# Preparing the next weight chunk ahead of emptying the PSUM banks, in three small projections of a two-block transformer kernel

## The reference

```python
def mla_qkv(c_q, c_kv, k_r, g_q, w_uq, g_kv, w_ukv, angles):
    q = (rmsnorm_2(c_q, g_q) @ w_uq).reshape(B, L, MLA_HEADS, MLA_NOPE + MLA_ROPE)
    kv = (rmsnorm_2(c_kv, g_kv) @ w_ukv).reshape(B, L, MLA_HEADS, MLA_NOPE + MLA_V)
    q_nope, q_rope = q[..., :MLA_NOPE], q[..., MLA_NOPE:]
    k_nope, v = kv[..., :MLA_NOPE], kv[..., MLA_NOPE:]
    ...
    q_rope = axial_rope(q_rope, *angles)
    k_rope = axial_rope(k_rope, *angles)
```

## Time and profile before

| | |
|---|---|
| profiled execution, its own time | 2443.72 us |
| its span in the profile | 2442.1 us |
| median of 3 runs | 2444.67 us |
| busy: TensorE matmul / VectorE / ScalarE | 98% / 73% / 48% of the span |
| stretch of `uk`, `uv`, `uq` | about 1430 to 1529 us |

### The profile page before, as it was taken

The page is one execution under the profiler, slowest core; times in us unless marked ns, Lnnn a source line. Parts: engine busy times, 40 slices in busy tenths (PEclk is TensorE's granted clock), DMA queues, the critical chain, the costliest instruction groups (busy, mean ns, idle before and its releaser), DMA issues.

```text
span 2442.1 us, 42380 instructions
## 1 busy us (share of the span) xinstructions
PE 2401.3 (98%) x14850; PEld 2135.9 (87%) x14850; DVE 1774.2 (73%) x2868; ACT 1165.0 (48%) x1671; POOL 0.2 (0%) x4
## 2 busy tenths in 40 slices
PE   8999999999999999999999999899999999999998
PEld 8998899988888888889988978588888888888887
DVE  5676678798878888889776455457777567766775
ACT  5344445554545654445523333345565444444453
POOL 0000000000000000000000000000000000000000
PEclk9999999999999999999999999999999999999999
DMA  7775567588778876787468522044556555555553
GB/s 271 278 274 183 185 221 245 176 291 290 260 248 281 289 271 231 271 282 239 162 238 280 193 70 69 26 164 152 192 181 198 185 185 180 195 184 185 192 187 132
DMA packets 142644, 508.97 MB, mean 208 GB/s; under 512 B 15824, under 2 KB 19408, under 8 KB 142160
## 3 DMA queue, kind: packets, MB, share of 16 engines
q1 hardware_dynamic: 142544, 507.60, 60.7%
HBM read 505.44 MB, written 2.10 MB: 208 GB/s over the span
## 4 chain that ended last, share of the span: by engine, by line
PE 96%; DVE 2%; ACT 1%; issue 0%; DMA 0%; DVEq 0%; SPq 0%; ACTq 0%
PE ps L1034 42%; PE ps L1036 20%; PE ps L1059 8%; PE ps L1060 8%; PE ps L1061 8%; PE ps L1385 1%; PE ps L1033 1%; PE ps L1089 1%; PE ps L1091 1%; PE ps L1090 1%; PE ps L1203 0%; PE ps L1395 0%; PE ps L1404 0%; PE ps L1185 0%; PE ps L1184 0%
## 5 line engine op out<-in xcount | busy, mean ns | idle before, releaser
L1512 DVE TENSOR_TENSOR lo<-raw,hi 128x1024 fp32r<-128x1024 f32 x754 | 916.0, 1222 | 437.3 <-ACT hi L557 434.9
L557 ACT ACTIVATE hi<-raw 128x1024 fp32r<-128x1024 f32 x754 | 795.8, 1059 | 818.4 <-PE ps L1036 465.4
L1034 PE MATMUL ps<-hs,hi 128*128 128x512 f32 x2880 | 1001.1, 394 | 2.4 <-DVE hs L1587 1.8
L1036 PE MATMUL ps<-hs,lo 128*128 128x256 f32 x2700 | 763.4, 283 | 0.0
L1034 PEld LDWEIGHTS ps<-hs,hi 128*128 128x128 f32 x2880 | 530.0, 188 | 113.6 <-issue 2.9
L1036 PEld LDWEIGHTS ps<-hs,lo 128*128 128x128 f32 x2700 | 508.6, 188 | 8.1
L1034 PE MATMUL ps<-hid,hi 128*128 128x512 f32 x1192 | 413.4, 394 | 0.0
L1036 PE MATMUL ps<-hid,lo 128*128 128x256 f32 x1114 | 314.6, 282 | 0.0
L1034 PEld LDWEIGHTS ps<-hid,hi 128*128 128x128 f32 x1192 | 218.8, 188 | 45.1
L1059 PE MATMUL ps<-xs,hi 128*128 128x258 f32 (+2 forms) x784 | 227.8, 291 | 10.9 <-DVE lo L1512 10.9
L1537 DVE SCALAR_TENSOR_TENSOR wm<-wm,cbx 128x1024 f32<-128x1024 f32 x192 | 234.0, 1219 | 5.2 <-DMA wm<-in_mod_stream 5.0
(11 more groups left out here) (314 smaller groups left out, 2952.4 us busy)
## 6 DMA issues: line engine op xcount, KB each, us to landing
raw<-in_stream SPq DMA_DIRECT2D x754, 512.0 KB, 4.2
wm<-in_mod_stream SPq DMA_DIRECT2D x192, 512.0 KB, 4.6
h<-in_tokens SPq DMA_DIRECT2D x4, 544.0 KB, 7.8
cx<-in_ctx_tokens SPq DMA_DIRECT2D x6, 256.0 KB, 5.8
out_tokens<-h SPq DMA_DIRECT2D x3, 512.0 KB, 2.9
cbx<-in_c_rows SPq DMA_DIRECT2D x1, 1024.0 KB, 12.1
cbc<-in_c_rows SPq DMA_DIRECT2D x1, 1024.0 KB, 5.4
na<-in_na_bias SPq DMA_DIRECT2D x1, 1024.0 KB, 4.8
```

What stands on the lines that cost most here:

```text
L557: act.activation(hi[:, slot, :], raw[:, slot, :], ACT.Copy).then_inc(hi_done, 1)
L1034: ins = pe.matmul(both, hi[:, slot, w], pair, start=kt == 0, stop=kt == last_k)
L1036: ins = pe.matmul(ps[:, bank, 0:NX], lo[:, slot, w], x_hi, start=False, stop=False)
L1512: dve.tensor_tensor(lo[:, slot, :], raw[:, slot, :], hi[:, slot, :].bitcast(F32), ALU.subtract)\
```

## The change

In the three layers `prepare` is moved ahead of the step that takes the results out of PSUM. On DVE this is so in `uk`, `uv` and `uq`, on ACT in `uq` (in `uk` and `uv` ACT takes no results of these layers out, and its order stays). Nothing is added or removed.

```diff
@@ ACT
             for hf in range(LY["uq"].halves):
+                prepare(LY["uq"], 0, hf)
                 second_halves(LY["uq"], 0, hf)
-                prepare(LY["uq"], 0, hf)
                 if hf == 0:
                     fourier_y(FN_GROUPS - 1)
@@ DVE
             def keys(hd):
 
+                prepare(LY["uk"], 0, hd)
                 dve.wait_ge(chunk_used, last_chunk(LY["uk"], 0, hd) + 5)
                 for t in range(2):
                     dve.tensor_copy(kn_m[:, 2 * hd + t, :], ps[:, 2 + t, :]).then_inc(bank_free, 1)
-                prepare(LY["uk"], 0, hd)
@@ DVE
             for g in range(FN_GROUPS):
+                prepare(LY["uv"], 0, g)
                 dve.wait_ge(chunk_used, last_chunk(LY["uv"], 0, g) + 5)
                 for t in range(4):
                     dve.tensor_copy(vt_m[:, t, g * HW:g * HW + HW], ps[:, t, 0:HW]).then_inc(bank_free, 1)
-                prepare(LY["uv"], 0, g)
```

## The result

The changed kernel takes 2459.89 us in the median of 5 runs (2454.96 to 2461.78); the kernel before took 2445.61 beside it (2443.72 to 2446.45, 5 runs). The ratio is 1.0057, 95% interval 1.0042 to 1.0072: slower by 14.3 us (10.3 to 17.6 by the interval), where 8 to 10 were forecast. The profiled execution took 2460.09, its span 2458.5.

A forecast was written before the change was run, and what follows sets the result against it. TensorE was taken to bound the kernel, for 96% of the span. Waits of 6.07 + 3.08 + 0 = 9.15 us on 2443.72 gave 2452.9, and with the median 0.95 higher 2453.8 us; range 2450.3 to 2457.3.

The forecast's parts named there:

- the steps: Four waits of TensorE for banks behind the halves of `uv`, the last before `uq`; 6.07 us in all.
- The swap matmuls: In `uq` they want both tiles of half 1; a stall of 0.44 us that doesn't add to the rest.
- half 5: Last half of `uq`, waiting for the first add of half 3; forecast to start 1.27 us later.
- the attention: Latent attention after `uq`, waiting for the last half's banks; start forecast 3.08 us later, the whole of `uq`.
- `uk` is 0 (0): Delay in `uk` covered by the next head's key matmuls, 0 us; rival of lost cover 3.4 us more, chance 0.05.
- given back: Rival: loads or splitting run ahead during the stall and TensorE catches up after 1588 us; fully, 2444.7 us; chance 0.05.
- the earlier `lo`: `lo` and the slot's next load come earlier; no credit taken; as a rival gain up to 5.7 us, chance 0.01.
- The clock falls once more: Rival: longer gaps in `uq` bring one more fall of TensorE's clock, 1.7 us, 2455.5 us in all; chance 0.20.
- Against it: the shorter gaps in `uq` of before, 1.53 and 1.26, brought none.: Argument against one more clock fall, from the kernel before's waits before half 5 and the latent attention.
- 6.07 + 3.08 + 0: Sum of the bank waits in `uv`, `uq` and `uk`: 9.15 us more.
- The prediction's own test: Prediction called wrong if the distance from the attention's start to the span's end changes by over 2 us.
- the base: Profiled execution of the kernel before, 2443.72 us, and the shown runs' median 0.95 above it, to which 9.15 was added.

The follow-up runs named there:

- e3: Kernel before with the new order in `uk` only; 2446.23 us, ratio 1.0000.
- e6: Changed kernel with 30 extra matmuls, product unread, filling TensorE's idle time before half 5, the latent attention and head 0's transposes; 2455.49 us, ratio 1.0041 to the kernel before.
- e4: The changed kernel again, unaltered, in a second session; 2457.54 us, 10.8 us more than the kernel before, ratio 1.0049.
- e7: Kernel before with the new order behind the last half of `uq` only, on ACT and DVE; 2449.68 us, ratio 1.0011.
- p3: One more profiled execution of the changed kernel, unaltered; 2459.93 us.
- p4: Another profiled execution of the changed kernel, unaltered; 2457.12 us.
- e5: Changed kernel with the old order behind the last half of `uq` only; 2453.61 us, ratio 1.0031 to the kernel before.
- p2: Another profiled execution of the kernel before, unaltered; 2443.50 us.
- p1: One more profiled execution of the kernel before, unaltered; 2444.52 us.
- b3: Kernel before with `uq` half 3's adds moved into DVE's rotation and `lo` of halves 3 to 5 put off behind the first latent softmax; 2443.01 us, ratio 0.9993.
- e1: Kernel before with the new order in `uv` only; 2451.16 us, ratio 1.0018.
- e0: The kernel before, unaltered, run as if it were a changed one; 2446.24 us, ratio 0.9999.
- b4: As b3, with 26 extra matmuls, product unread, before the attention, before head 0's transposes and around the ffn2 spread; 2441.89 us, ratio 0.9985 to the kernel before.
- b1: Kernel before with the adds of `uq` half 3 moved from behind DVE's rotation into its middle; 2445.66 us, ratio 0.9995.
- e2: Kernel before with the new order in `uq` only, on ACT and DVE; 2449.93 us, ratio 1.0015.

## Why the prediction was wrong

**What held.** `prepare` stands with its full length in front of the banks. In `uv` the steps are 1.56, 1.03, 1.33 and 1.90, forecast 1.55, 1.12, 1.41 and 1.99. The swap matmuls come 0.43 later (0.44), half 5 1.24 (1.27), the attention 3.13 (3.08). `uk` is 0 (0), shown by e3. The sum is 8.95 in the profile after and 8.97 by e6, against 9.15. Nothing was given back and nothing gained by the earlier `lo`.

**What failed: the clock among the rivals.** "The clock falls once more" was right in kind, and it had 0.20 and 1.7 us. The step that failed is the sentence "Against it: the shorter gaps in `uq` of before, 1.53 and 1.26, brought none." It weighs gaps that the changed kernel no longer has. The two new gaps, 2.24 and 3.13 us, are both longer than the 1.96 us which the same paragraph shows to bring a fall; the evidence was for the rival. So the sum 6.07 + 3.08 + 0 has no term for the clock at all. The rival was under-priced as well: 1.7 is one fall, and behind 3.13 us the clock stayed low for longer and fell again at head 0 in after, e4, e7 and p3 (4.69 in e7, with that gap alone), or fell once in half 5 and once in the attention (p4). e5 takes that gap away, and the cost at the attention goes, though a fall behind the 2.24 us gap costs 1.56 in its place; e6 fills the gaps, and all of it goes while the waits stay. By the four profiles of each kernel the term is 3.3 us, not 0 and not 1.7. The stretch as a whole is thus 9.0 + 3.3 = 12.3 us. The prediction's own test, that the distance from the attention to the end of the span changes by no more than 2 us, fails too: 2442.1 - 1529.38 = 912.7 before, 2458.5 - 1542.37 = 916.1 after.

The Trainium skill (TensorE: Matmul & The Clock Gate, Part 1: The HAM clock gate) says that the array drops to half clock after idleness, that work brings it back, and that how many matmuls run at the low clock differs between runs of one kernel. e5, e6 and e7 agree with the first two, and p2 against p1 (0.03 and 1.72 us) with the third. The fall near 1203 us in after isn't of that kind in the record: PE is busy for 3.00 of 3.00 us there.

**What failed beside it: the base.** The sum was put on one profiled execution and its median of three, as if only the change could move the rest. Executions differ by up to 4.3 us in when `uv` starts (1472.9 in b3, 1477.2 after), mostly through the clock's falls near 1204 and 1375 us, and the execution that I used as base had an early one. It came from the smaller group: of the 76 executions of the kernel before that ran beside the e and b runs, 26 took under 2445 us and 50 over 2445.5. A range that was 3.5 us wide to each side left that out. 12.3 us on 2445.61 is 2457.9, above the range even so. The first session gave 14.3 more than before, the second 10.8; the 12.3 lie between, and inside both intervals.

**What stays open.** All six profiles with the new order in `uk` and `uv` had a late start of `uv`, 1475.4 or later, and of the eleven others five. Before the falls near 1204 and 1375 us the instructions are the same, and e3 and e1, with one of the two changes each, started early. Six of six may be chance, since two thirds of the executions of the kernel before are in the slower group. But no run settles whether the two kernels, started in turn, meet the clock differently, and no run compares chips (three were used: one for e0 to e3, e7, b3 and b4, one for e4 to e6 and b1, one for p1 to p4). The first session's 2 us over the 12.3 are put down to that scatter; this is argued, not shown.

## What to carry to other kernels

When the work that frees an accumulator and the preparation of later data wait for the same event, do the freeing first: here the preparation has four halves of time, and in `uv` the bank has only what the Fourier matmuls cover. What is put ahead of the freeing costs what isn't covered: 5.8 us of 4 x 2.23 in `uv`, 3.1 in `uq`, nothing in `uk`. The same reasoning the other way round, with the splits moved to where nobody waits, makes the stretch 1.76 us shorter (b3), and with the gaps filled as well the kernel is 4.0 us faster than before (b4).

A wait on TensorE costs its length and then what the clock does behind it: here the waits cost 9.0 us and the clock 3.3. Line up the new gaps with those that did and didn't bring a fall, and compare the new lengths, not the old ones. Where a gap can't be closed, matmuls that nobody reads can keep the clock (e6, b4).

Before a forecast of a few us is put on one profiled execution, see how its falls of the clock lie; a few of them were worth as much as a third of the whole change.

## What the hardware showed that I had not expected

- The same gap of 1.96 us on the same instructions brought a fall in before, e0, e3 and p1, but none in p2, e1, e5 and b3. The gap of 2.24 us brought one in e5, p3 and p4, none in after, e2 and e4. A gap of 3.13 us brought one in all six profiles that had it idle, and attention to head 1 took 1.4 to 4.7 us more than at full clock there.
- The clock falls although TensorE is recorded as busy. In the profile after it runs matmuls with one column (L1124, 128x1) from 1201.0 to 1205.7 us; they slow down from 1203.2 on, and PE busy is 3.00 of 3.00 us over 1203 to 1206 at a granted clock of 0.55. The same goes for L1100, one column too, from 1374.2 to 1378 us, where the clock falls between 1376 and 1378. How much of it is due to the single column was not tried.
- The 30 extra matmuls of e6 left the clock at 1.00 in the stretch, but its five executions had 1.5 to 2.7 us around the span where the others have 1.6 (b4, with 26, had 1.6 to 2.3), which takes back part of what they give. I have no explanation.
